# Forget gates as plain fp32 products in column groups, with a reordered first unit, in a two-layer encoder kernel

## The reference

```python
def rmsnorm(x, g):
    return x * rsqrt(mean(x * x, axis=-1) + EPS) * g

def even_mixer(h, ...):
    z = h @ w_in
    u, g, q, k, v, f_logit = split(z)              # f_logit: one column for each of 8 heads
    a = silu(rmsnorm(causal_depthwise_conv(u * sigmoid(g), conv_w) + conv_b, conv_norm))
    q, k = rmsnorm(q, q_norm), rmsnorm(k, k_norm)  # per head of 64
    log_f = log_sigmoid(f_logit + b_f)
    o = forgetting_attention(q, k, v, log_f)       # logits + cumsum(log_f)_i - cumsum(log_f)_j, causal
    return concatenate([a, o]) @ w_out

def reference(x, ...):                             # x: 1 x 512 x 1024, float32
    for layer in range(2):
        x = x + 0.5 * swiglu(rmsnorm(x, ffn1_norm[layer]), ...)    # hidden width 2816
        h = rmsnorm(x, mix_norm[layer])
        x = x + (even_mixer(h, ...) if layer == 0 else odd_mixer(h, ...))
        x = x + 0.5 * swiglu(rmsnorm(x, ffn2_norm[layer]), ...)
    return x
```

## Time and profile before

| | |
|---|---|
| time, median of 3 runs | 1849.33 us (1849.28 to 1849.39) |
| the profiled execution | 1849.31 us, its span 1847.5 us |
| PE matmul | busy 1835.4 us, 99% |
| PE weight loads | 1504.5 us, 81% |
| DVE | 824.3 us, 45% |
| ACT | 633.2 us, 34% |
| POOL | 356.7 us, 19% |
| PE's granted clock | 1.00 over the span |
| HBM | 174.85 MB moved, 94 GB/s |

### The profile page before, as it was taken

One profiled execution on the slowest core, in us unless ns is written; L12 is line 12 of the kernel. 1 busy time (PEld: TensorE's weight loads), 2 busy tenths in 40 slices (PEclk: granted clock), 3 DMA queues, 4 the chain that ended last, 5 costly groups with the idle time before them and its releaser, 6 DMA issues.

```text
span 1847.5 us, 22267 instructions
## 1 busy us (share of the span) xinstructions
PE 1835.4 (99%) x8269; PEld 1504.5 (81%) x8269; DVE 824.3 (45%) x934; ACT 633.2 (34%) x833; POOL 356.7 (19%) x295
## 2 busy tenths in 40 slices
PE   8999999999999999999999999999999999999999
PEld 7888888888668888888888888888888888888887
DVE  6343433368856443443344343333455544343321
ACT  5333322247765333332233333222212333333221
POOL 5111111129853111111111111011213221111000
PEclk9999999999999999999999999999999999999999
DMA  5333343233104333333323333432333333333331
GB/s 162 103 91 102 91 125 94 77 80 92 35 24 126 101 93 98 95 114 105 88 79 95 99 93 100 121 94 81 92 91 103 91 102 92 102 91 110 108 111 35
DMA packets 341403, 174.85 MB, mean 95 GB/s; under 512 B 6304, under 2 KB 340332, under 8 KB 341356
## 3 DMA queue, kind: packets, MB, share of 16 engines
q1 hardware_dynamic: 337100, 172.12, 32.2%
q10 hardware_dynamic: 4256, 2.11, 0.4%
HBM read 172.10 MB, written 2.10 MB: 94 GB/s over the span
## 4 chain that ended last, share of the span: by engine, by line
PE 93%; DVE 4%; ACT 2%; issue 1%; POOL 0%; ACTq 0%; DVEq 0%; POOLq 0%
PE bank L1324 30%; PE bank L1326 30%; PE bank L1325 30%; DVE w_lo L964 1%; DVE conv L1000 1%; ACT w_hi L645 1%; ACT tap_prod L804 0%; PE bank L1530 0%; DVE neg_max L1180 0%; PE bank L1546 0%; ACT probs_a L857 0%; PE bank L1465 0%; DVE k_n L1129 0%; PE bank L1515 0%; DVE q_n L1129 0%
## 5 line engine op out<-in xcount | busy, mean ns | idle before, releaser
L964 DVE TENSOR_TENSOR w_lo<-raw,w_hi 128x1024 fp32r<-128x1024 f32 (+2 forms) x308 | 408.5, 1327 | 697.0 <-ACT w_hi L645 696.5
L1324 PE MATMUL bank<-xg_hi,w_hi 128*128 128x512 f32 x1728 | 673.8, 390 | 2.7 <-DVE w_lo L964 2.6
L1326 PE MATMUL bank<-xg_hi,w_lo 128*128 128x512 f32 x1728 | 672.3, 389 | 0.0
L1325 PE MATMUL bank<-xg_lo,w_hi 128*128 128x512 f32 x1728 | 672.3, 389 | 0.0
L645 ACT ACTIVATE w_hi<-raw 128x1024 fp32r<-128x1024 f32 (+2 forms) x308 | 339.9, 1104 | 775.6 <-PE bank L1326 775.5
L1324 PEld LDWEIGHTS bank<-xg_hi,w_hi 128*128 128x128 f32 x1728 | 324.3, 188 | 72.7 <-DVE w_lo L964 3.1
L1326 PEld LDWEIGHTS bank<-xg_hi,w_lo 128*128 128x128 f32 x1728 | 324.3, 188 | 67.6
L1325 PEld LDWEIGHTS bank<-xg_lo,w_hi 128*128 128x128 f32 x1728 | 324.4, 188 | 66.9 <-issue 0.2
L545 POOL TENSOR_TENSOR scaled<-acted,rstd 128x512 f32<-128x512 f32 x92 | 118.8, 1291 | 835.9 <-ACT acted L722 787.9
L1324 PE MATMUL bank<-h_hi,w_hi 128*128 128x512 f32 x704 | 274.5, 390 | 0.0
L1326 PE MATMUL bank<-h_hi,w_lo 128*128 128x512 f32 x704 | 274.0, 389 | 0.0
(11 more groups left out here) (193 smaller groups left out, 991.9 us busy)
## 6 DMA issues: line engine op xcount, KB each, us to landing
raw<-in_ffn_w_gate SPq DMA_DIRECT2D x88, 512.0 KB, 3.8
raw<-in_ffn_w_up SPq DMA_DIRECT2D x88, 512.0 KB, 3.8
raw<-in_ffn_w_down SPq DMA_DIRECT2D x64, 704.0 KB, 4.5
raw<-in_od_w_in SPq DMA_DIRECT2D x24, 512.0 KB, 3.7
raw<-in_ev_w_in SPq DMA_DIRECT2D x20, 512.0 KB, 3.8
raw<-in_ev_w_out SPq DMA_DIRECT2D x16, 256.0 KB, 2.8
raw<-in_od_w_out SPq DMA_DIRECT2D x8, 512.0 KB, 3.9
x_rows<-in_x SPq DMA_DIRECT2D x4, 512.0 KB, 6.7
```

The costliest lines, as they stand in the source:

```text
L964: dve.tensor_tensor(w_lo[:, u % 2, c0:c0 + n], raw[:, u % 4, 0:n], raws(w_hi[:, u % 2, c0:c0 + n]), ALU.subtract).then_inc(wlo_ready, 1)
L1324: pe.matmul(dst, a[0], b[0], start=start, stop=False)
L1325: pe.matmul(dst, a[0], b[1], start=False, stop=False)
L1326: return pe.matmul(dst, a[1], b[0], start=False, stop=stop)
```

## The change

1. **Gates.** `wf_hi` and `wf_lo` go, with their work on ACT, DVE and POOL. POOL makes `wf_gain`, 8 tiles of 32 columns (8 of them filled: weight times gain), and `same_head`, a 128 x 128 matrix of ones where row and column are the same modulo 32 (a memset and 7 selects). PE multiplies the unsplit x by `wf_gain` in plain fp32, tile k into column group k mod 4, so that four partial sums lie in the four quarters of bank 5. ACT copies the bank to SBUF, and after unit 7 PE makes one plain product of `same_head` and the copy: the sum of the four quarters, in each of them.
2. **First unit.** ACT splits unit 0 before the first square; squares 2 to 7 come after the split of unit 1. DVE splits unit 0 before the first copy, and two of the copies that were ahead of unit 1's split come after it. The copies and squares go through the tiles in the order 0, 1, 2, 5, 6, 7, 3, 4; before units 1 to 3 PE waits for the copies 4, 5 and 6, which empty the banks of these units. The product with ones moves into unit 2, ahead of its fifth tile.
3. **Fans.** The last four fans come in pairs, after (1, 2) and (2, 0).
4. **Taps and values.** Three of DVE's taps fewer ahead of the last `qk_scale`, one fewer at step 1 of attention, one more at each of the steps 3 to 6. `value(3)` is ahead of `maxima(1)`.

```diff
@@ -175 +175 @@
     TURN_BANKS = (1, 2, 3, 4, 5)
+    COPIES = [0, 1, 2, 5, 6, 7, 3, 4]
     first_rows = at("first_rows", [FIRST, P], f32, H + TB * D * 4)
@@ -183 +184 @@
     v = at("v", [P, TB, ATT], f32, VAT)
-    wf_hi, wf_lo = at("wf_hi", [P, KD, P], f32r, VAT), at("wf_lo", [P, KD, P], f32r, VAT + KD * P * 4)
+    F_COLS = P // 4
+    wf_gain, same_head = at("wf_gain", [P, KD, F_COLS], f32, VAT), at("same_head", [P, P], f32, VAT + KD * F_COLS * 4)
     CAT = VAT + 2 * TB * ATT * 4
@@ -238 +240 @@
     assert sum(TAPS_A) + TAPS_NEXT + TAPS_QK[0] == TAPS
-    TAPS_V, TAPS_T = [2, 2, 2, 2, 2, 3, 4], 0
+    TAPS_V, TAPS_T = [2, 2, 3, 3, 3], 1
     ACT_TAPS_A, ACT_TAPS_NEXT, ACT_TAPS_QK, ACT_TAPS_V = [3, 4, 4, 3], 5, [4, 3, 4, 4, 3, 4, 3, 3], [3, 3, 4, 5, 0]
@@ -254 +256 @@
-    QK_FANS, V_SUMS, V_FANS = {6: 0, 7: 2}, (0, 0), [(1, 2), (1, 3), (2, 0), (2, 1)]
+    QK_FANS, V_SUMS, V_FANS = {6: 0, 7: 2}, (0, 0), {(1, 2): AB, (2, 0): AB + 2}
     V_SCORES = [(2, 3), (3, 2)]
@@ -324 +326 @@
         step = sem("step")
-        wf_cleared, wfhi_ready, wflo_ready, f_done = (
-            sem("wf_cleared"), sem("wfhi_ready"), sem("wflo_ready"), sem("f_done"))
+        wf_ready, same_ready, f_parts, f_copied, f_done = (
+            sem("wf_ready"), sem("same_ready"), sem("f_parts"), sem("f_copied"), sem("f_done"))
         col_done, col_ready = sem("col_done"), sem("col_ready")
@@ -355 +357 @@
-        def gate_cols(tensor):
-            return tensor[:, :, :].rearrange("p k (r c) -> p k r c", r=4)[:, :, :, 0:HEADS]
         def out_unit(g, u):
@@ -582 +580 @@
                     pool.wait_ge(unit_done, ph.unit0)
-                    pool.memset(raws(wf_hi[:, :, :]), 0.0).then_inc(wf_cleared, 1)
-                    pool.memset(raws(wf_lo[:, :, :]), 0.0).then_inc(wf_cleared, 1)
+                    pool.memset(wf_gain[:, :, :], 0.0).then_inc(wf_ready, 1)
+                    pool.memset(same_head[:, :], 0.0).then_inc(same_ready, 1)
+                    pool.wait_ge(wf_arrived, 16 * 5)
+                    pool.wait_ge(vec_ready, 2)
+                    pool.wait_ge(wf_ready, 1)
+                    gains = vec[:, GAIN_COL[ph.norm]:GAIN_COL[ph.norm] + KD]
+                    pool.tensor_tensor(wf_gain[:, :, 0:HEADS], wf_raw[:, :, :],
+                                       gains.unsqueeze(2).broadcast_to([P, KD, HEADS]), ALU.mult).then_inc(wf_ready, 1)
+                    for n in range(7):
+                        pool.wait_ge(same_ready, n + 1)
+                        pool.affine_select(out=same_head[:, :], in_=same_head[:, :], compare_op=ALU.not_equal, fill=1.0,
+                                           base=(n - 3) * F_COLS, pattern=[[-1, P]], channel_multiplier=1)\
+                            .then_inc(same_ready, 1)
                 if ph.kind == "pair":
@@ -662 +671 @@
-            def first_square(j):
-                act.wait_ge(x_new, j + 1)
-                if j >= 2:
-                    act.wait_ge(sq_added, j - 1)
-                act.activation(sq[:, j % 2, :], x[:, j, :], ACT.Square).then_inc(sq_ready, 1)
+            def first_square(n):
+                act.wait_ge(x_new, n + 1)
+                if n >= 2:
+                    act.wait_ge(sq_added, n - 1)
+                act.activation(sq[:, n % 2, :], x[:, COPIES[n], :], ACT.Square).then_inc(sq_ready, 1)
@@ -699 +708 @@
                             split_hi(ph, g, 4)
-                        if ph is A_GATE and first and u == 3:
-                            act.wait_ge(wf_arrived, 16 * 5)
-                            act.wait_ge(wf_cleared, 2)
-                            act.activation(gate_cols(wf_hi), wf_raw[:, :, :].unsqueeze(2).broadcast_to([P, KD, 4, HEADS]),
-                                           ACT.Copy).then_inc(wfhi_ready, 1)
+                        if ph is A_GATE and not first and u == 3:
+                            act.wait_ge(f_parts, 1)
+                            act.activation(lf[3][:, :], bank[5][:, :], ACT.Copy).then_inc(f_copied, 1)
                         if first and u == 0:
@@ -865 +872 @@
                 first_high(j)
+            split_hi(phases[0], 0, 0)
             first_square(0)
-            split_hi(phases[0], 0, 0)
             for j in (2, 3):
                 first_high(j)
+            first_square(1)
             for j in range(4, KD):
-                first_square(j - 3)
                 first_high(j)
             split_hi(phases[0], 0, 1)
-            for j in (KD - 3, KD - 2, KD - 1):
+            for j in range(2, KD):
                 first_square(j)
@@ -1012 +1019 @@
                         f, half = g * 2 + u // 2, u // 2
-                        if ph is A_GATE and not first and u == 0:
-                            dve.wait_ge(wfhi_ready, 1)
-                            dve.tensor_tensor(gate_cols(wf_lo),
-                                              wf_raw[:, :, :].unsqueeze(2).broadcast_to([P, KD, 4, HEADS]),
-                                              raws(gate_cols(wf_hi)), ALU.subtract).then_inc(wflo_ready, 1)
                         if not (first and u in (1, 2)):
@@ -1188 +1189 @@
                 qk_scale(4)
+                qk_scale(5)
                 conv_taps(TAPS_V[2])
-                qk_scale(5)
-                conv_taps(TAPS_V[3])
                 split_lo(ph, 0, 3)
                 qk_scale(6)
-                conv_taps(TAPS_V[4])
                 qk_scale(7)
-                conv_taps(TAPS_V[5])
+                conv_taps(TAPS_V[3])
@@ -1211 +1210 @@
                         value(1)
-                        conv_taps(TAPS_V[6])
+                        conv_taps(TAPS_V[4])
+                        value(3)
                         maxima(1)
-                        value(3)
                     if 2 <= t < PAIRS:
@@ -1221 +1220 @@
                                           ALU.subtract).then_inc(olo_ready, 1)
-                    if t >= 2:
+                    if t >= 3:
                         conv_taps(TAPS_T, late=t >= LAST_IN_BANK)
@@ -1239 +1238 @@
-            def first_copy(j):
+            def first_copy(n):
+                j = COPIES[n]
                 dve.tensor_copy(x[:, j, :], bank[TURN_BANKS[j % len(TURN_BANKS)]][:, :]).then_inc(x_new, 1)
@@ -1248 +1248 @@
                 first_low(j)
+            split_lo(phases[0], 0, 0)
+            for j in (0, 1):
                 first_copy(j)
-            split_lo(phases[0], 0, 0)
-            for j in range(2, KD):
+            for j in (2, 3):
                 first_low(j)
-                if 3 <= j < KD - 1:
-                    first_copy(j - 1)
+            first_copy(2)
+            for j in range(4, KD):
+                first_low(j)
+            first_copy(3)
             split_lo(phases[0], 0, 1)
-            for j in (KD - 2, KD - 1):
-                first_copy(j)
+            for n in range(4, KD):
+                first_copy(n)
@@ -1358 +1361 @@
                         hook = None
-                        if first and ph is phases[0] and u == 0:
-                            hook = turn_in
+                        if first and ph is phases[0] and u:
+                            pe.wait_ge(x_new, u + 3)
+                        if first and ph is phases[0] and u in (0, 2):
+                            hook = late_squares if u else turn_in
                         projection(ph, g, u, wait_x=first and u == 0, before=hook)
...
-                            pe.wait_ge(wflo_ready, 1)
+                            pe.wait_ge(wf_ready, 2)
                             for k in range(KD):
-                                last = product(bank[5][:, :], (wf_hi[:, k, :], wf_lo[:, k, :]),
-                                               (xg_hi[:, k, :], xg_lo[:, k, :]), k == 0, k == KD - 1)
-                            last.then_inc(f_done, 1)
+                                rows = slice(k % 4 * F_COLS, (k % 4 + 1) * F_COLS)
+                                last = pe.matmul(bank[5][rows, :], wf_gain[:, k, :], x[:, k, :], start=k < 4, stop=k >= 4)
+                            last.then_inc(f_parts, 1)
+                        if ph is A_GATE and not first and u == 3:
+                            pe.wait_ge(same_ready, 8)
+                            pe.wait_ge(f_copied, 1)
+                            pe.matmul(bank[5][:, :], same_head[:, :], lf[3][:, :], start=True, stop=True).then_inc(f_done, 1)
                         if first and u == 1 and ph is phases[0]:
-                            sum_squares(ph)
                             pe.wait_ge(first_ready, 1)
@@ -1392 +1401 @@
                 pe.matmul(bank[6][:, :], ones_r[:, :], sum_lo[:, :], start=False, stop=True).then_inc(ssq_done, 1)
+            def late_squares(k):
+                if k == KD // 2:
+                    sum_squares(phases[0])
@@ -1655 +1669 @@
                             elif (u, tb) in V_FANS:
-                                fan(AB + V_FANS.index((u, tb)))
+                                fan(V_FANS[u, tb])
```

(1 more changed line is left out.)

## The result

The changed kernel takes 1853.57 us in the median, the kernel before 1849.32 us: ratio 1.0021, 95% interval 1.0015 to 1.0028. That is 4.2 us slower, 0.6 us above the upper end of the range. The executions of before lie within 0.12 us of each other. Those of the changed kernel (18) lie in groups: one at 1851.25, six at 1852.5 to 1852.6, eight at 1853.3 to 1853.8, three at 1854.2 to 1854.6. A nineteenth execution took 2635.70 us at a mean granted clock of 0.654 over its span and is left out of the groups and of the ratio. The mean granted clock over the span, recorded for each execution, goes with the groups: 1.000 for the one at 1851.25, 0.999 for the six, 0.998 for the other eleven. The profiled one took 1853.32 us, for a span of 1851.5 us.

A forecast was written before the change was run, and what follows sets the result against it. PE, 93% of the last-ending chain, bounds the kernel, so only its standing time or needless products can be won. Start +2.1, gates -0.05, attention -0.8 sum to +1.25: 1850.6 us, range 1845.6 to 1853.0.

The forecast's parts named there:

- start: First 40 us: earlier first units against a new PE wait before unit 2 and later units; +2.1 us, bounds +1.0 and +3.
- gates: Gate phase: 3.4 us won at unit 7, given back as 2.5 waiting for ACT's copy and 0.9 of sum; -0.05 us.
- fans, values, taps: Fans and attention: earlier first scores, but POOL's taps hold back the third scores; -0.8 us, bounds -2.2 and +0.5.
- rival (b): Clock falls after PE's waits at 23.9 and 421.6 us, about 2.1 us lost each time: 1854.8 us; chance 0.06.
- The first product and unit 1: Start: first product at about 9.8 instead of 11.38, unit 1 at 18.3 instead of 19.83; by itself -1.5 us.
- The new wait: Before unit 2: w_hi behind squares that wait for POOL's additions; unit 2 at about 26.9, PE standing 3 us.
- The rule weighed in the prediction: Gate passes: loads overlap running products only when the row group differs; gates would cost +0.9 instead of -0.05 us.
- Fans: Last four fans issued in pairs: two visits fewer on PE, -1.25 us.
- POOL's taps: Attention: POOL adds taps before scaling odd probabilities; PE ready at 499.6 transposes at 501.3, third scores 501.8 instead of 503.09.
- (a): All gains come through at start, gates and attention: -6.2 us, 1843.1 us; chance 0.13 for all or most of it.
- (c): Gates: column groups don't run side by side, passes take 6.9 us instead of 1.7; +4.3, 1854.9 us; chance 0.03.
- (d): Gates: loads of the 16 passes lie in the open, 1.6 us, partly hidden; +0.9, 1851.5 us; chance 0.03.

The follow-up runs named there:

- start alone: The kernel before with only the changed start (first units' splits, copies and squares): median 1853.01 us, ratio 1.0019; lowest group 1851.8 to 1851.9.
- gates alone: The kernel before with only the changed forget gates: median 1851.19 us, ratio 1.0006; lowest group 1849.12 to 1849.18.
- attention alone: The kernel before with only the changed fans, taps and value order: median 1848.90 us, ratio 1.0000; lowest group 1848.8 to 1848.9.
- all three busy: The changed kernel with small unused products on PE in its waits before unit 2, the sum over groups and the odd transposes: median 1851.16 us, ratio 1.0010.
- all mended: The changed kernel with unit 2's w_hi behind square 3, POOL's constants behind the gates, ACT's copy earlier, two POOL taps moved into attention: median 1848.51 us, ratio 0.9996.
- without the gates: The kernel before with changed start (w_hi earlier, POOL's constants later) and changed fans, taps, values (two POOL taps later), old forget gates: median 1848.86 us, ratio 0.9998.
- w_hi ahead alone: The changed kernel with w_hi of unit 2 on ACT behind square 3 in place of square 7: median 1854.03 us, ratio 1.0024.

## Why the prediction was wrong

The forecast was +1.25 us; without falls of the clock the change measures +1.9, with them +4.2 in the median. Of the 3.0 us by which the forecast was low, 2.4 are falls and 0.6 are sizes.

| term | forecast | without falls | from |
|---|---|---|---|
| start | +2.1 | +2.5 | start alone, lowest group |
| gates | -0.05 | -0.1 | gates alone, lowest group |
| fans, values, taps | -0.8 | -0.4 to -0.6 | attention alone; all three busy: 2.4 late at rstd, 1.8 at the end |
| falls of the clock | 0 | (+2.4) | changed kernel against all three busy |

- **The step that failed** is the term for the clock, which the sum puts at nothing. The forecast priced the waits that the change makes at their length alone and left the fall of the clock behind them to rival (b), with a chance of 0.06. The runs show such a fall in most executions, +2.4 us in the median. The mechanism of (b) was right. It was set aside on the one wait of 1.7 us with the clock at 1.00 behind it. One instance of a shorter wait says nothing about a longer one, and the forecast itself created three waits of 1.7 to 3 us. The third, before the odd transposes, was in the forecast's own working (PE ready at 499.6, transposes at 501.3) and missing from the rival. The Trainium skill (TensorE: Matmul & The Clock Gate, section Why this matters for your kernels), cited beside that rival, warns of gaps in which PE is idle; the trace agrees in kind, with clocks of 0.67, 0.68 and 0.66 in the stretches behind waits of 2.9 (start alone), 2.2 and 1.87 us, and adds that it happens in some executions and not in others.
- **The price in (b)**, 2.1 us a fall, fits the gates' fall (2.05). The other two measure 1.2 and 0.9. At the start this is because part of what is lost lies where PE waits anyway (1.55 us at unit 3, 1.2 at unit 6); for the third wait the same reason is an argument. The price was taken from the slow transposes before 6.8 us, where the profile gives a granted clock of 1.00, so no row ties that pace to the clock, and that it fits one fall of three is in part luck. (b)'s time, 1854.8, lies above all 18 executions.
- **The first product and unit 1** were right: 9.79 and 18.33, forecast 9.8 and 18.3.
- **The new wait** was right in place, cause and size: unit 2 at 27.06 (forecast 26.9), PE idle for 2.85 (3). The start without falls is 0.4 more than forecast: in the run with all three waits busy unit 4 starts at 39.35, 2.0 late as forecast, unit 5 at 45.05, 2.3 late, and unit 6 2.4 late (50.63 against 48.22), so the forecast's 0.15 for what comes behind unit 4 was the term too small: it measures 0.4.
- **The gates** were right: passes side by side in 1.85 us (forecast 2.0), the copy behind w_hi, a wait of 2.28 (2.5), nothing won. The rule weighed in the prediction (the Trainium skill, TensorE: Matmul & The Clock Gate, section Part 3: Packing small matmuls), by which the loads would lie in the open, does not show: 16 passes of 0.43 in four groups make 1.72 of the 1.85, so 16 loads of some 0.1 us can't be in it besides. The forecast did not see that a copy in good time would have brought little either (0.35 us, all mended against without the gates), since DVE bounds the units behind.
- **Fans** were right: from the first pair to the first scores 8.14 us (all three busy: 484.80 to 492.94) against 10.35 before, 0.88 of it the old wait and 1.3 the two visits fewer (forecast 1.25).
- **POOL's taps** bound as forecast: odd transposes at 505.47, that is 501.3 + 3.8 and 0.4. The 0.4 is the head start of 0.35 us that the forecast gave POOL's chain and that does not show: with all three waits busy POOL scales the odd probabilities 2.41 us late (502.45), PE's transposes of rstd being 2.44 late. Counted from these, the third scores start 0.9 us earlier than before (504.65 against 503.09), where 1.3 was forecast.
- Rivals (a), (c) and (d) are out: no execution of the changed kernel below 1851.25, groups side by side, loads hidden.

## What to carry to other kernels

A forecast that creates a wait of PE owes two prices: the wait, and a stretch at the lower clock behind it in a part of the executions, 0.9 to 2.1 us each here. Times of a kernel that fall into groups, where the kernel before has one, are the sign of it, and small products without use in the wait tell the two prices apart in one run. A gain in one stage is worth what the next stage's slowest engine lets through: ask at what time that engine's last conversion lands, not only whether PE waits for it today.

## What the runs showed of the hardware

- The granted clock falls behind waits of PE of 1.9 to 2.9 us in some executions: start alone, wait 2.9, clock 0.67 in the stretch from 25 to 30 us; gates alone, wait 2.2, clock 0.68 in the stretch behind it; attention in the changed kernel, wait 1.87, clock 0.66. From 28.3 to 31.3 us of the changed kernel it is 0.50, and products follow each other at 0.43 instead of 0.23 us. Behind waits of the same length it stayed 1.00 in others (2.28 in the changed kernel's profile, 1.9 in that of the attention part alone, both at 1.00). The kernel before, whose longest waits are 2.5 us ahead of its first work and 1.7 at 11.38, had one execution about 1 us above the rest (1850.21) among 33 in one comparison, and none in the others.
- In each of the ten falls that the traces hold, the missing share of the clock adds up to 1.70 to 1.75 us, whatever the wait ahead of it (changed kernel, start: 5 x 0.19 + 5 x 0.15; gates alone: 5 x 0.02 + 5 x 0.32). The time lost by it is 0.9 to 2.1 us.
- With small fp32 products of 128 columns on otherwise idle PE the profiled execution shows 1.00 behind all three waits; the mean clock over the span is 1.000 in ten of the 11 executions and 0.999 in one, whose time (1851.21) is that of the others.
- An addition on POOL of 1.30 us took 2.12 and 2.18 when it ran beside a w_lo on DVE, as one did in the earlier trace rows; a select on POOL of 0.34 took 1.02 beside DVE's w_lo of unit 4 (w_hi ahead alone, at 36.21).
